# Fourier mixer folded and first transformed during the projection, and next tiles put into the drain of the rotated heads

## The reference

```python
h = layer_norm(x) * (1 + scale) + shift
q, k, v, g_a, cu, cb, cc, g_c, fu, g_f = split(h @ w_in)   # 512,128,128,512, then 6 x 256
y_attn = attention(axial_rope(rms(q)), axial_rope(rms(k)), v) * silu(g_a)   # 8 heads of 64, 2 kv heads
y_conv = cb * short_conv(cc * cu) * silu(g_c)
f = fft2(fu, over tokens and within groups of 64, ortho).real ; y_four = (f @ f_mix) * silu(g_f)
x = layer_norm(ALPHA * x + (1 + gate) * (concat(y_attn, y_conv, y_four) @ w_out)) * ln_g + ln_b
```

## Time and profile before

| what | value |
| --- | --- |
| median of 3 executions | 3526.44 us (3525.18 to 3528.34) |
| the profiled execution, its own time | 3525.79 us |
| its span in the trace | 3524.0 us |
| mean granted clock of TensorE, share of full speed | 0.962 |
| 2561 to 2604 (Fourier stage, layer 0): TensorE busy, clock | 24.72 of 43.00 us, 0.76 |
| 3182 to 3225 (the same, layer 1): TensorE busy, clock | 24.43 of 43.00 us, 0.76 |

### The profile page before, as it was taken

How to read it: one execution, slowest core, us unless ns; L and a number is a source line. 1 busy time by engine, 2 the same in 40 slices (tenths; PEclk the granted TensorE clock), 3 DMA queues, 4 the chain that set the end, 5 groups by cost and what they waited for, 6 DMA issues and landing times. The chain is left out here.

```text
span 3524.0 us, 39583 instructions
## 1 busy us (share of the span) xinstructions
PE 3298.1 (94%) x16038; PEld 2695.9 (77%) x16038; DVE 2087.2 (59%) x2663; ACT 1301.4 (37%) x1874; POOL 397.3 (11%) x498
## 2 busy tenths in 40 slices
PE   6999999999998779999999999889979999997999
PEld 3788888878786668878888888767858786785887
DVE  7555555564753879665655555562258885225886
ACT  3222222232231158532222222542147763213772
POOL 0000000021011122110001001001011200101120
PEclk8999999999998789999999999999989999998999
DMA  4222222216443068412232222124163212416421
GB/s 194 95 85 77 91 72 94 86 60 112 147 167 139 25 96 102 78 46 84 84 104 87 73 95 96 44 72 125 64 121 63 57 61 72 123 66 120 64 58 60
DMA packets 137093, 313.46 MB, mean 89 GB/s; under 512 B 55144, under 2 KB 72332, under 8 KB 125904
## 3 DMA queue, kind: packets, MB, share of 16 engines
q1 hardware_dynamic: 75680, 215.51, 19.5%
q0 software_dynamic: 61232, 95.42, 12.8%
HBM read 258.71 MB, written 52.19 MB: 88 GB/s over the span
## 5 line engine op out<-in xcount | busy, mean ns | idle before, releaser
L2024 DVE TENSOR_TENSOR w_lo<-w_raw,w_hi 128x1024 fp32r<-128x1024 f32 (+1 forms) x131 | 218.7, 1669 | 359.4 <-ACT w_hi L1467 359.4
L833 PE MATMUL psum<-a_hi,w_hi 128*128 128x512 f32 x704 | 276.8, 393 | 5.3 <-DVE a_lo L2146 3.8
L833 PE MATMUL psum<-a_hi,w_lo 128*128 128x512 f32 x704 | 275.4, 391 | 0.0
L833 PE MATMUL psum<-a_lo,w_hi 128*128 128x512 f32 x704 | 275.2, 391 | 0.0
L2517 DVE TENSOR_TENSOR attn_tl<-psum,attn_th 128x512 fp32r<-128x512 f32 x384 | 247.4, 684 | 24.8 <-ACT attn_th L1782 21.3
L1236 PEld LDWEIGHTS psum<-mats,attn_num 128*128 128x128 f32 x1536 | 168.9, 144 | 110.3 <-ACT attn_num L1791 109.2
L1782 ACT ACTIVATE attn_th<-psum 128x512 fp32r<-128x512 f32 x384 | 209.6, 597 | 115.1 <-PE psum L1236 108.1
L1467 ACT ACTIVATE w_hi<-w_raw 128x1024 fp32r<-128x1024 f32 (+1 forms) x131 | 183.8, 1403 | 174.6 <-PE psum L833 45.9
L1236 PE MATMUL psum<-mats,attn_num 128*128 128x128 f32 x1536 | 215.2, 284 | 33.7 <-ACT attn_num L1791 33.2
L2214 DVE SCALAR_TENSOR_TENSOR x<-psum,cols,x 128x1024 f32<-128x1024 f32 x144 | 184.3, 1282 | 94.0 <-PE psum L833 93.8
L2511 DVE TENSOR_REDUCE attn_sm<-psum 128x1 f32<-128x1024 f32 x128 | 156.1, 1220 | 29.8 <-PE psum L1226 29.8
(11 more groups left out here) (566 smaller groups left out, 8456.5 us busy)
## 6 DMA issues: line engine op xcount, KB each, us to landing
w_raw<-in_w_ada SPq DMA_DIRECT2D x52, 1024.0 KB, 5.0
w_raw<-in_w_gu SPq DMA_DIRECT2D x44, 1024.0 KB, 4.9
w_raw<-in_w_in SPq DMA_DIRECT2D x34, 1024.0 KB, 5.0
w_raw<-in_w_down SPq DMA_DIRECT2D x22, 1024.0 KB, 5.0
w_raw<-in_w_out SPq DMA_DIRECT2D x12, 1024.0 KB, 8.5
qk_hi_scratch<-p_out_hi POOLq DMA_DIRECT2D x18, 512.0 KB, 3.0
qk_lo_scratch<-p_out_lo POOLq DMA_DIRECT2D x18, 512.0 KB, 3.8
w_early<-in_w_ada SPq DMA_DIRECT2D x8, 1024.0 KB, 18.1
```

What stands on the lines that cost most here:

```text
L833: mm = e.matmul(bank, a[:, k * width + m * P:k * width + (m + 1) * P], b(k, h), start=(ends[0] and k == order[0] and i == 0), stop=(ends[1 ...
L2024: e.tensor_tensor(like(src, lo), src, like(src, hi.bitcast(F32)), ALU.subtract).then_inc(*w_done.mark(n, part))
```

## The change

- TensorE: tile 6 and then tile 7 of the projection are put around the transposes of v and the last rotation; the first Fourier products go ahead of tile 21. In the attention the pairs for transposes and results are taken at units 1 and 3, not at the start.
- VectorE: the fold is made when block 7 is fetched; the alternating sum follows tile 20, in place; the convolution's last step (`conv_end(1)`) goes behind the low parts of the transformed u; the gated results come after the second maximum of the attention.
- ScalarE: the convolution's last factor (`last_factor(1)`) goes behind the first rounding; the fences before the stage and before the attention are gone, and one wait for TensorE's end of the projection is left.
- Both: the fetch of `("dft", l, 1)`, which prepares the first output block, moves to unit 4 of the attention.
- Loads: u, signs, gates and the first heads go between POOL's stores, SP's `fourier` is gone.
- Memory: odd parts and signs live in `t.acc` and `sq`, other tiles are laid out so that the early ones overlap nothing in use.

```diff
-                m.odd = sb(f"fo{l}_odd", [P, 2, HALF], F32, sc)
-                m.row = sb(f"fo{l}_row", [P, 2, P], F32, sc)
+                m.odd = t.acc[:].rearrange("p (g c) -> p g c", g=2)
+                m.alt = t.sqh[0]
                 m.uh = sb(f"fo{l}_uhi", [P, 2, ST // 2, 256], F32R, sc)
                 m.ul = sb(f"fo{l}_ulo", [P, 2, ST // 2, 256], F32R, sc)
+                m.row = sb(f"fo{l}_row", [P, 2, P], F32, sc)
+                gap(f"fo{l}", 35 * 1024, sc)
+                m.gf = sb(f"fo{l}_g", [P, 2, S], F32, sc)
...
-    u_in, g_in = loaded("fo_u_in", "SP", 2), signal("fo_g_in", "SP", 16)
+    u_in, g_in, alt_in = loaded("fo_u_in", "POOL", 2), signal("fo_g_in", "POOL", 16), signal("fo_alternating_in", "POOL", 16)
...
-            p_t = ps.take(e, (name, "t"), num_lo, name, n - 1, 1)
-            p_o = ps.take(e, (name, "o"), res_done, name, n // 4 - 1)
...
+                if u == 1:
+                    p_t = ps.take(e, (name, "t"), num_lo, name, n - 1, 1)
+                if u == 3:
+                    p_o = ps.take(e, (name, "o"), res_done, name, n // 4 - 1)
...
+            def plain(nt, block_):
+                n_, whi, wlo = block_
+                key, what, tl = ("in2", l, nt), (nt - 14) % 4, (nt - 14) // 4
+                emptied = (rope_act, "raw", key) if nt < 6 else (staged, key) if nt < 14 else \
+                    ((conv_act, "u", l, tl), (conv_dve, "cu", l, tl), (conv_dve, "cb", l, tl), (conv_act, "g", l, tl))[what]
+                gemm(key, nt % 2, KT, whi, wlo, hi, lo, *emptied, block_end=n_ if nt % 2 else None)
...
+            block_ = block(("in2", l, 3))
+            plain(6, block_)
+            p = ps.take(e, ("v2", l), out_lo, key)
+            e.wait_ge(*rope_act.at("raw", key))
+            for j in range(ST):
+                mm = e.transpose(p.full[:, j * P:(j + 1) * P], m.tmp[1][0][:, j * P:(j + 1) * P], ident)
+            mm.then_inc(*v_turned.mark(l))
+            step(pending)
+            plain(7, block_)
             while pending:
                 step(pending)
             here("PE", f"proj2b{l}")
...
+            for b in range(4, 11):
+                block_ = block(("in2", l, b))
+                for nt in (2 * b, 2 * b + 1):
+                    if nt == 21:
+                        e.wait_ge(*four_act.at("table", l))
+                        for g in range(2):
+                            p = ps.take(e, ("fo u", l, g), four_dve, "u", l, g)
+                            e.wait_ge(*four_dve.at("folded", l, g))
+                            for j in range(ST // 2):
+                                for part, src in enumerate((m.even, m.odd)):
+                                    mm = e.matmul(p.full[:, j * 256 + part * P:j * 256 + (part + 1) * P],
+                                                  src[:, g, j * P:(j + 1) * P], ab[:, g, part * P:(part + 1) * P],
+                                                  start=True, stop=True)
+                            mm.then_inc(*four_pe.mark("u", l, g))
+                    plain(nt, block_)
...
-            ab = sqh[1].rearrange("p (g c) -> p g c", g=2)
-            e.wait_ge(*four_act.at("table", l))
-            for g in range(2):
-                p = ps.take(e, ("fo u", l, g), four_dve, "u", l, g)
-                e.wait_ge(*four_dve.at("folded", l, g))
-                for j in range(ST // 2):
-                    for part, src in enumerate((m.even, m.odd)):
-                        mm = e.matmul(p.full[:, j * 256 + part * P:j * 256 + (part + 1) * P], src[:, g, j * P:(j + 1) * P],
-                                      ab[:, g, part * P:(part + 1) * P], start=True, stop=True)
-                mm.then_inc(*four_pe.mark("u", l, g))
             p = ps.take(e, ("fo middle", l), four_dve, "out middle", l, 1)
...
+                if u == 4 and not masked:
+                    blocks.get(("dft", tag[1], 1))
...
+            def last_factor(tl):
+                key = ("in2", l, 17 + 4 * tl)
+                e.wait_ge(*tile_done.at(*key))
+                e.wait_ge(*conv_dve.at("cu", l, tl))
+                e.activation(m.cu[:], ps.of[key].full, ACT.Silu).then_inc(*conv_act.mark("g", l, tl))
...
+                    elif what == 3 and tl == 0:
+                        last_factor(0)
+            e.wait_ge(*passed("PE", f"fourier{l}"))
...
-            blocks.get(("dft", l, 1))
+            blocks.get(("dft", l, 0))
+            last_factor(1)
...
-            fence(f"attn2_{l}")
+            here("ACT", f"attn2_{l}")
             attention(f"attn2_{l}", f"mix2{l}", m, ("out2", l), False)
...
+                if u == 1 and early is not None:
+                    early()
+                if u == 4 and not masked:
+                    blocks.get(("dft", tag[1], 1))
...
+            def conv_end(tl):
+                j = 8 + tl
+                e.wait_ge(*st_stored[j % 4].at(f"p2b{l}", j - 4))
+                e.wait_ge(*conv_act.at("g", l, tl))
+                e.wait_ge(*conv_dve.at("cb", l, tl))
+                e.tensor_tensor(m.st[j % 4][:], m.ac[:], m.cu[:], ALU.mult).then_inc(*conv_dve.mark("out", l, tl))
...
+            def fold():
+                for g in range(2):
+                    e.wait_ge(*u_in[g].at(l))
+                    e.tensor_copy(m.even[:, g, 0:1], m.fu[:, g, 0:1]).then_inc(*four_dve.mark("first", l, g))
+                    e.memset(m.odd[:, g, 0:1], 0.0).then_inc(*four_dve.mark("zero", l, g))
+                    e.tensor_tensor(m.even[:, g, 1:HALF], m.fu[:, g, 1:HALF], m.fu[:, g, back], ALU.add).then_inc(
+                        *four_dve.mark("even", l, g))
+                    e.tensor_tensor(m.odd[:, g, 1:HALF], m.fu[:, g, 1:HALF], m.fu[:, g, back], ALU.subtract).then_inc(
+                        *four_dve.mark("folded", l, g))
+
             for b in range(3, 11):
                 blocks.get(("in2", l, b))
+                if b == 7:
+                    fold()
...
-            fence(f"fourier{l}")
-            for j in range(6, 10):
-                e.wait_ge(*st_stored[j % 4].at(f"p2b{l}", j))
...
+                    elif what == 3 and tl == 0:
+                        conv_end(0)
...
-            e.wait_ge(*g_in.at(l))
-            for g in range(2):
-                e.wait_ge(*four_dve.now())
-                e.tensor_tensor_reduce(out=sqh[0], in0=m.even[:, g, :], in1=m.alt[:], scale=1.0,
+                if g == 0:
+                    e.wait_ge(*alt_in.at(l))
+                e.wait_ge(*four_pe.at("u", l, g))
+                e.tensor_tensor_reduce(out=m.even[:, g, :], in0=m.even[:, g, :], in1=m.alt, scale=1.0,
                                        scalar=m.fu[:, g, HALF:HALF + 1], op0=ALU.mult, op1=ALU.add,
                                        accum_out=cols[:, 40 + g:41 + g]).then_inc(*four_dve.mark("alternating", l, g))
-            blocks.get(("dft", l, 0))
+            here("DVE", f"fourier{l}")
             for g in range(2):
                 hi, lo = (v[:, g, :, :].rearrange("p a b -> p (a b)") for v in (m.uh, m.ul))
                 e.wait_ge(*four_act.at("u", l, g))
                 e.tensor_tensor(lo, ps.of[("fo u", l, g)].full, hi.bitcast(F32), ALU.subtract).then_inc(*four_dve.mark("u", l, g))
-            blocks.get(("dft", l, 1))
+            blocks.get(("dft", l, 0))
             e.wait_ge(*four_pe.at("middle", l))
...
+            conv_end(1)
...
-                e.wait_ge(*four_dve.now())
-                e.tensor_tensor(m.fu[:, g, 0:HALF], m.even[:, g, :], m.gf[:, g, 0:HALF], ALU.mult).then_inc(
...
-            fence(f"attn2_{l}")
-            attention(f"attn2_{l}", f"mix2{l}", m, ("out2", l), False)
+
+            def gated_results():
+                for g in range(2):
+                    e.wait_ge(*four_dve.at("back", l, g))
+                    e.tensor_tensor(m.fu[:, g, 0:HALF], m.even[:, g, :], m.gf[:, g, 0:HALF], ALU.mult).then_inc(
+                        *four_dve.mark("out forth", l, g))
+                    e.tensor_tensor(m.fu[:, g, back], m.odd[:, g, 1:HALF], m.gf[:, g, back], ALU.mult).then_inc(
+                        *four_dve.mark("out", l, g))
+                here("DVE", f"attn2_{l}")
+                for j in (8, 9):
+                    e.wait_ge(*st_stored[j % 4].at(f"p2b{l}", j))
+
+            attention(f"attn2_{l}", f"mix2{l}", m, ("out2", l), False, gated_results)
...
-            e.wait_ge(*passed("PE", f"fourier{l}"))
-            first_heads(at_name, m.at)
+                if j == 3:
+                    for g in range(2):
+                        e.wait_ge(*st_stored[g].at(f"p2b{l}", g))
+                        e.dma_start(m.fu[:, g, :], d.proj[6 + g]).then_inc(*u_in[g].mark(l))
+                if j == 4:
+                    e.wait_ge(*four_pe.at("table", l))
+                    e.dma_start(m.alt, ins["alternating"]).then_inc(*alt_in.mark(l))
+                if j == 5:
+                    first_heads(at_name, m.at)
+                if j == 8:
+                    for g in range(2):
```

(17 more changed lines are left out.)

90 lines of the change are left out of this document (25 added, 65 removed).

## The result

| | before | after |
| --- | --- | --- |
| median | 3525.81 us (3525.16 to 3528.34, 4 runs) | 3490.93 us (3489.29 to 3495.66, 4 runs) |
| ratio, with its 95% interval | 1 | 0.9902 (0.9885 to 0.9919) |
| the profiled execution, its own time | 3525.79 us | 3495.66 us |
| its span | 3524.0 us | 3493.9 us |
| mean granted clock of TensorE | 0.962 | 0.965 |

The change takes 34.9 us off by the medians; 37.0 was forecast. The profiled execution of the changed kernel is the longest of its four, so by the two profiles the difference is 30.1 us.

The account below looks back on a forecast made before the run. TensorE, busy 94% of the span, was taken to bound the kernel, so only its waits and lower clock could give time. 38.2 + 7.2 - 13.2 + 4.8 = 37.0 us off the 3526.4 median gives 3489.5, range 3474 to 3501.

Parts of the forecast that it names:

- Loads and fold for nothing: Fourier stage: the fold and its loads, placed beside projection products, were costed at nothing.
- The slower rival: Fourier stage: u's load on POOL lands late and delays VectorE; at 100 us the time is 3540; chance 0.02.
- the rival that they would not: First Fourier products: some wait holds the fold until the projection ends, giving 3525 to 3529 us; chance 0.03.
- T0 to T1 of 16.2 us: From the last projection tile's end to the last Fourier product's end: 38.5 us in layer 0 becomes 16.2.
- Releases 2.5 us: After the last projection tile: u's eviction by ScalarE and its low part on VectorE, with releases, take 2.5 us.
- 1.4 us or less: TensorE before the Fourier transform: the one pause left there is 1.4 us or less, with full clock after it.
- an upper bound only: Clock loss after the pause before the transform: taken as none, bounds 0 and 1.3 us a layer.
- Start of the attention: First exponential starts 3.6 us earlier, up to 1 us late afterwards: 7.2 us gained in two layers, bounds 4 and 8.
- The weight block at unit 4: Attention: rounding the first output block at unit 4 costs 6.6 us a layer, 13.2 us lost; bounds 3.5 and 8.
- cheap-unit-4 rival: Attention, unit 4: only the plain wait is paid, 3.5 instead of 6.6 us a layer, 3483 us; chance 0.15.
- Rotated heads: Tile 6 fills waits of 5.5 and 2.0 us, but a new wait precedes tile 8; gain 4.8 us.
- The clock spared: Four new pauses, before tile 8 and at unit 4, keep full clock: 7.6 us less, 3482 us; chance 0.07.

Follow-up runs that it names:

- fence_late: Changed kernel with ScalarE's wait for the last heads and stores moved ahead of tile 14, VectorE's ahead of the fold: 3475.59 us, ratio 0.9859.

## Why the prediction was right

3489.5 was forecast and 3490.9 measured, inside 3474 to 3501 and faster as given. That the two are 1.4 us apart is partly luck: by the tally the Fourier stage gave 4.8 us less than forecast, and the start of the attention, unit 4 and the rotated heads came out 0.4, 1.0 and 1.1 better, which leaves 34.7 of the 37.0; before stood 0.6 lower beside the changed kernel than the 3526.4 that the forecast starts from. By the steps:

- **What bounds it.** Right. The latency named in the earlier trace rows went, and TensorE's busy time hardly moved (3298.1 and 3294.1 us).
- **Loads and fold for nothing.** Right: u's loads, issued at 2432.1, landed 6.0 and 6.6 us later, and the fold stood at 2478.9. The slower rival, u's load late, had 40 us to spare. All 16 products went early, so the rival that they would not fell too.
- **T0 to T1 of 16.2 us.** Too good by 2.4 us a layer, the largest miss. "Releases 2.5 us" was 3.5: the eviction and then both of VectorE's low parts (1.03 + 2.36). That made the pause 2.3 us and not "1.4 us or less", and in this profile both layers then ran at half clock, the 1.3 us that I kept as an upper bound only. That bound held, but the 1.0 us of the releases lay outside it. 33.4 us were gained instead of 38.2, with the early products counted.
- **What the early products are worth.** The sum charged them 3.6 us and looked no further. It did not ask what the layer would be with the fold early and the products late: 2.8 us a layer better.
- **Start of the attention.** 7.6 by the tally and 7.7 by undoing it, 7.2 forecast.
- **The weight block at unit 4.** 12.2 lost by the tally, 12.4 by undoing it, 13.2 forecast. Its exponentials 5 and 6 came 8.4 and 12.1 us behind exponential 4, where 8.7 and 12.4 were counted. The cheap-unit-4 rival fell.
- **Rotated heads.** 5.9 by the tally, 5.4 by undoing it, 4.8 forecast. The new wait was 5.1 us in layer 0 as counted (5) but 5.2 in layer 1, not 7: the last head's store took 4.11 us there against 3.84, and was not the 2 us later that I had carried over from the earlier trace rows. The half clock after it was priced at 2.0 by unit 8's transposes, which are few; 48 products of tile 8 lost 2.9. The two errors cancelled by luck: 1.8 us less wait in one layer against 0.9 more half clock in each.
- **The clock spared.** This rival named a real thing and no full case. Of the pauses that it means, none was spared: in every layer that had them, with the tiles where the changed kernel has them, it took 14.0 to 14.9 us from tile 8's start to the table's move (11.8 in fence_late, without the pause), and 11.7 to 12.5 from exponential 4 to 6 (5.9 without the block), with the transposes behind the pause at half clock each time. Only the fall at the transform was missing, in 3 of 12.
- **Left open.** 1.2 and 1.8 us were lost between exponential 12 and the last. They lie at exponentials 31, 39 and 47, whose gaps vary from 2.9 to 4.4 us between profiles of kernels that do not differ there, before included; no cause was looked for.

## What to carry to other kernels

When work moves early, ask what holds its result: the early products here only waited for memory that the next tile still read, and either a layout in which the split may follow at once or leaving them late was better. A filled bubble is worth only what the next wait leaves of it, so follow the filled engine to its next semaphore, and where that is a fence, ask which bytes it protects and move it to the first write of them. And a block of work that was free in a drain, beside products that don't need its engines, cost 6.2 us in a pipeline whose engines have little room (TensorE, VectorE and ScalarE busy 98, 90 and 79% from 2640 to 2720 in the changed kernel), where its own work is 1.9 and 2.3 us.

## What the hardware showed that was not expected

- The same instructions with all of the second block's tiles 544 bytes a partition higher took 11.5 us more: 0.233 instead of 0.227 us a product of 128x512, at a granted clock of 1.00. In the two pairs of kernels that also had the new layout it was 16.7 and 16.0 us.
- A pause of 2.3 us of TensorE ended at half clock in 6 of 12 layers; in 3 the clock fell 0.5 to 1.0 us behind it, and in 3 not at all.
- Profiles of kernels with the same instructions up to there differ by up to 6.5 us at v's move in layer 0, so a difference of two spans is no measure of a part worth 5 us.
